# Two transformer blocks on one core: six input slabs and the output projection of the first block in three fp32r passes

## The reference

```
hn = rms_norm(x, norm1_g)
proj = hn @ w_in                      # 1024 x 2304: qa 512, ka 128, va 128, qb 512, kb 512, vb 512
qa, ka = rope(rms_norm(qa)), rope(rms_norm(ka));  qb, kb = rms_norm(qb), rms_norm(kb)
out_a = global_gqa_attention(qa, ka, va)
out_b = dilated_mixture_attention(qb, kb, vb)
mixed = concat([rms_norm(out_a), rms_norm(out_b)])
x = x + mixed @ w_out                 # 1024 x 1024
x = x + conv_ffn(rms_norm(x, norm2_g), w_up, conv_w, conv_b, w_down)
```

## Time and profile before

| | |
|---|---|
| median of 3 runs | 2467.14 us (2466.2 to 2467.89) |
| profiled execution | 2466.14 us, span 2464.4 us |
| mean granted TensorE clock | 0.992 |
| PE busy | 2393.4 us, 97% |
| PEld busy | 2044.9 us, 83% |
| POOL busy | 1603.4 us, 65% |
| DVE busy | 1093.4 us, 44% |
| ACT busy | 1068.3 us, 43% |

### The profile page before, as it was taken

One profiled execution on the slowest core, in us unless ns is written; L12 is line 12 of the kernel. 1 busy time (PEld: TensorE's weight loads), 2 busy tenths in 40 slices (PEclk: granted clock), 3 DMA queues, 4 the chain that ended last, 5 costly groups with the idle time before them and its releaser, 6 DMA issues.

```text
span 2464.4 us, 37279 instructions
## 1 busy us (share of the span) xinstructions
PE 2393.4 (97%) x14828; PEld 2044.9 (83%) x14828; DVE 1093.4 (44%) x2091; ACT 1068.3 (43%) x1987; POOL 1603.4 (65%) x1364
## 2 busy tenths in 40 slices
PE   8999999999999999999999999999998999989998
...
GB/s 219 179 176 193 167 118 126 103 81 195 267 95 131 120 129 119 128 103 180 103 69 103 100 89 103 99 96 98 119 227 122 120 129 136 111 186 158 172 203 137
DMA packets 379311, 339.42 MB, mean 138 GB/s; under 512 B 14448, under 2 KB 343698, under 8 KB 378130
## 3 DMA queue, kind: packets, MB, share of 16 engines
...
q0 software_dynamic: 576, 0.43, 0.2%
...
HBM read 329.62 MB, written 7.61 MB: 137 GB/s over the span
## 4 chain that ended last, share of the span: by engine, by line
PE 87%; POOL 4%; DVE 3%; ACT 2%; issue 2%; DMA 2%; SPq 0%; ACTq 0%; POOLq 0%; DVEq 0%
PE PS L751 41%; PE PS L1167 13%; PE PS L1176 5%; PE PS L809 5%; PE PS L1367 3%; POOL rounded L2824 3%; PE PS L774 3%; PE PS L1224 2%; PE PS L702 2%; PE PS L1081 1%; PE PS L1208 1%; PE PS L1285 1%; PE PS L973 1%; PE PS L1069 1%; DMA ring<-in_w_down_dram 1%
## 5 line engine op out<-in xcount | busy, mean ns | idle before, releaser
L2824 POOL TENSOR_TENSOR rounded<-ring,rounded 128x512 fp32r<-128x512 f32 (+1 forms) x872 | 1115.8, 1313 | 485.0 <-ACT rounded L1419 371.6
L751 PE MATMUL PS<-rounded 128*128 128x256 f32 (+1 forms) x6096 | 1048.1, 334 | 15.7 <-DVE mid_a L2529 5.0
L751 PEld LDWEIGHTS PS<-rounded 128*128 128x128 f32 x6096 | 929.9, 191 | 129.8 <-issue 13.6
L2847 POOL TENSOR_TENSOR rounded<-ring,constants 128x512 fp32r<-128x512 f32 x216 | 230.9, 1099 | 236.4 <-PE PS L751 113.4
L1167 PE MATMUL PS<-rounded 128*128 128x512 f32 (+1 forms) x1536 | 346.8, 382 | 2.3 <-DVE mid_a L2580 1.8
L1167 PEld LDWEIGHTS PS<-rounded 128*128 128x128 f32 x1536 | 274.4, 189 | 58.1 <-issue 6.4
L1419 ACT ACTIVATE rounded<-ring 128x2048 fp32r<-128x2048 f32 (+1 forms) x99 | 180.1, 1823 | 123.9 <-DMA ring<-in_w_mlp_dram 44.4
L2566 DVE SCALAR_TENSOR_TENSOR mid_a<-PS,V,mid_a 128x510 f32<-128x510 f32 (+3 forms) x256 | 182.6, 713 | 71.5 <-ACT mid_a L1764 64.6
L1176 PE MATMUL PS<-rounded 128*128 128x512 f32 (+1 forms) x768 | 140.8, 340 | 0.0
L2029 ACT ACTIVATE PS<-PS 128x512 f32<-128x512 f32 (+1 forms) x64 | 30.4, 475 | 251.7 <-DVE PS L2737 251.6
L1176 PEld LDWEIGHTS PS<-rounded 128*128 128x128 f32 x768 | 117.9, 189 | 18.1 <-issue 3.6
...
## 6 DMA issues: line engine op xcount, KB each, us to landing
ring<-in_w_mlp_dram SPq DMA_DIRECT2D x64, 1024.0 KB, 5.3
ring<-in_w_in_dram SPq DMA_DIRECT2D x56, 1024.0 KB, 5.5
ring<-in_ada_w_dram SPq DMA_DIRECT2D x48, 1024.0 KB, 5.3
...
ring<-in_w_ssd_o_dram SPq DMA_DIRECT2D x16, 1024.0 KB, 5.9
ring<-in_w_out_dram SPq DMA_DIRECT2D x12, 1024.0 KB, 5.0
```

Source lines behind the costliest of these rows:

```text
L751: mm = pe.matmul(PS[:, b, 0:cols], w[:, k, m * P:(m + 1) * P], x(half * kt + k), start=(half == 0 and k == 0 and n_pass == 0), stop=(half ...
L2824: ins = pool.tensor_tensor(lo[:, r], raw[:, r], hi[:, r], ALU.subtract)
L2847: ins = pool.tensor_tensor(hi[:, r], raw[:, r], ones[:, 0:1].broadcast_to([P, 512]), ALU.mult)
```

## The change

The six slabs 4 to 9 of `w_in` go in three passes. POOL splits them by the second form, with two hi buffers in `mid_a`. The normed input is split as well: ACT rounds its eight pieces (`lat_hi`), DVE subtracts (`lat_lo`), and PE waits for these. The four slabs of `w_out` go in three passes too: ACT rounds two of them inside the attention loop, after `exp1` of units 13 and 15, and two in the projection, at k = 1 and 3; POOL subtracts. The turned attention output is rounded by ACT (`mix_hi`), and DVE subtracts (`mix_lo`), which is now what frees the PSUM bank of a transpose. The first two `w_up` slabs are rounded at k = 4 and 5 in place of 3 and 5. A `w_up` slab is free when `split_ready` stands at 10 more than before.

The diff, cut to its core:

```
@@ PE
-            to_features(4, lat, SEQ, act_freed, begin=False, end=False)
+            in_parts = dict(rest=lambda k: lat_lo[:, k, :], hi_at=in_at)
+            pe.wait_ge(*c.need(lo_ready, KT))
+            to_features(4, lambda k: lat_hi[:, k, :], SEQ, act_freed, begin=False, end=False, **in_parts)
...
-            to_tokens(1, 256, LT, act_freed)
+            to_tokens(1, 256, LT, act_freed, parts=(lat_hi, lat_lo), hi_at=in_at)
...
-            to_features(4, lambda k: mix1[:, k, :], SEQ, dve_freed, after=one_behind(hT, SEQ),
-                        first_rows=lambda: pe.wait_ge(*c.need(turned_freed)))
+            def later_mix(k):
+                if k >= KT - 4:
+                    pe.wait_ge(*c.need(turned_freed))
+            to_features(4, lambda k: mix_hi[:, k, :], SEQ, dve_freed, after=one_behind(hT, SEQ), rest=lambda k: mix_lo[:, k, :],
+                        hi_at=out_at, last_rows=later_mix)
@@ ACT
+            for k in range(KT):
+                act.wait_ge(*c.need(scaled))
+                act.activation(lat_hi[:, k, :], hT[:, k, 0:SEQ], ACT.Copy).then_inc(*c.made(hi_ready))
...
             for u in range(n_u + 1):
                 if u < n_u:
                     exp1(u)
+                if u in (n_u - 3, n_u - 1):
+                    round_slab(outs, (u - n_u + 3) // 2, out_at)
                 if u >= 1:
                     weightsT(u - 1, 512)
...
-                turned_to(mix1[:, f, :], SEQ, col("outa_norm_g", f) if f < 4 else col("outb_norm_g", f - 4))
+                turned_to(mix_hi[:, f, :], SEQ, col("outa_norm_g", f) if f < 4 else col("outb_norm_g", f - 4), hi_ready)
...
             for k in range(KT):
+                if k in (1, 3):
+                    round_slab(outs, 2 + k // 2, out_at)
                 square_of_tile(k, hT, SEQ)
-                if k in (3, 5):
-                    round_slab(ups, k // 2 - 1, up_at)
+                if k in (4, 5):
+                    round_slab(ups, k - 4, up_at)
@@ DVE
+            settle(scaled)
+            for k in range(KT):
+                rest_of(lat_lo[:, k, :], hT[:, k, 0:SEQ], lat_hi[:, k, :])
...
             scale_half(1)
+            bank4[0] = 0
+            for f in range(KT):
+                rest_of_turned(mix_lo[:, f, :], mix_hi[:, f, :], col("outa_norm_g", f) if f < 4 else col("outb_norm_g", f - 4), SEQ)
@@ POOL
+            split(range(s0, s0 + 4), in_at)
+            split(range(s0 + 4, s0 + 6), in_at)
+            rests(range(first_slab["out"], first_slab["out"] + 4), out_at)
             rests(up_slabs, up_at, body=FFT, lo_at=(FFT // 2) * up_rest_at)
@@ SP
-                booked((split_ready, j + 1), 2, (tile_ready, total[0] + 2 * (j + 1)))
+                booked((split_ready, 10 + j + 1), 2, (tile_ready, total[0] + 2 * (j + 1)))
```

16 lines of the change are left out of this document (12 added, 4 removed).

## The result

| | before | changed kernel |
|---|---|---|
| median | 2466.67 us (2462.93 to 2467.89) | 2491.16 us (2483.49 to 2499.04) |
| profiled execution | 2466.14 us, span 2464.4 us | 2490.01 us, span 2488.2 us |
| mean granted TensorE clock | 0.992 | 0.984 |

The ratio is 1.0103 [1.0087, 1.0119]: 24.5 us slower between the medians, 21 to 29 by the interval. I had forecast 11.2 us slower, and at most 18. The direction is right, the size is not. A second measurement of the same kernel gave 2489.32 us and 1.0085 [1.0068, 1.0102], so it is not one odd run.

A forecast was written before the change was run, and what follows sets the result against it. PE was taken as the bound, with POOL's 9.2 us pitch now setting the input's end. Input +11.2, attention +3.4, turn +1.15, projection -4.6 made +11.15 us on 2466.14: 2477.3 profiled, 2478.3 median, range 2474.5 to 2485.

The forecast's parts named there:

- POOL sets the end of the input slabs: Input slabs 4 to 9: POOL splits one per 9.2 us, PE needs 5.76 and waits; slab 9 ends 10.3 us later.
- The second chain, by DVE's rotation: Input stage: DVE's rope after slab 7 makes the first maximum at least 9.9 us late, even with slabs 8 and 9 free.
- The waits and the low clock in the input: Input slabs: PE's waits bring 1.2 GHz stretches, costing nothing in the middle, 0.9 us (0 to 1.7) behind the last wait.
- The rule that I cited: Trainium skill: matmul bursts shorter than the operand wait start at the lower clock, so each of six input slabs begins slow.
- ACT's rounding in the attention, 3.4: Attention loop: ACT's rounding of slabs 22 and 23 delays unit 13 and later, last output 3.4 us late (1.9 to 4.6).
- The attention loop as a whole: Attention loop: ACT's rounding of two slabs was the only cost, 3.4 us.
- rival 1: Input slabs: DVE-POOL port costs more than rope rows show, or clock stays low; +17.5 us, 2484.7 (clock: 2483); chance 0.12.
- The turn, +1.15: Turning the attention output: transposes' banks now wait for DVE's subtractions, costing 1.15 us, at most 1.9.
- The projection, -4.6: Output projection: three-pass tiles take 25.8 us in place of 30.4, a gain of 4.6; 3 with waits.
- What follows is shifted as a whole: Everything behind the projection runs on PE and its own waits, moved in time with no change in length.
- the five cases: Whole kernel: the forecast (0.70, 2475 to 2482) and four rivals at 2484.7 (0.12), 2475.4 (0.10), 2481 (0.05), 2460 (0.03).
- Slower: Whole kernel: slower than before by more than the measurable 0.2%, some 5 us; chance 0.95.

The follow-up runs named there:

- e6: Kernel before with only the input slabs in three passes, ACT rounding and POOL only subtracting, four hi buffers, projection in float32: 2465.68 us, 0.9992.
- e3: Changed kernel plus unused matmuls on PE in the waits for the six input splits: 2484.51 us, 1.0072.
- e9: The changed kernel measured again, unchanged: 2489.32 us, 1.0085.
- e7: e2 with POOL's subtractions held until the attention output is scaled, ACT's roundings staying in the loop: 2471.16 us, 1.0013.
- e14: e2 plus 5, 0 and 4 unused matmuls on PE ahead of the weight transposes of units 13, 14 and 15: 2464.11 us, 0.9995.
- e2: Kernel before with only the output projection in three passes, input slabs in float32: 2470.01 us, 1.0024.
- e1: Kernel before with only input slabs 4 to 9 in three passes, output projection in float32: 2478.63 us, 1.0045.

## Why the prediction was wrong

- **POOL sets the end of the input slabs: right for the first profile, and a little dearer.** I had six pitches of 9.2 and 1.2 us for DVE, split at 102.0, 54.6 us behind the first sum of squares. It was 99.85 - 43.29 = 56.6. A start of POOL well before 45 was to be a sign that I was wrong. It began at 42.05, but the first sum of squares was 4.1 us early as well; in the second profile it began at 45.83. Against the first sum of squares it was 0.6 us later than I had it, and its six splits took 57.8 us for 56.4. The two last lines of POOL in the input stage:

```profile
88.24 5.83 POOL L2874 TENSOR_TENSOR rounded<-ring,constants 128x512 fp32r<-128x512 f32 x4
94.14 5.71 POOL L2851 TENSOR_TENSOR rounded<-ring,rounded 128x512 fp32r<-128x512 f32 x4
```

  DVE's rope cost the hi of slab 9 1.8 us and its lo 0.7, not 1.2 over both. With that the stage is 13.1 us longer, for 11.2. e6 shows that the pitch was the main bound: with 5.2 us in place of 9.6 the whole loss is gone. The second chain, by DVE's rotation, I had at 9.9 us against 10.3 and gave it no price. (I had compared the end of the last pair of heads, 108.6, with the old first maximum; like with like it is 10.4, a tie.) In the second profile it ended last, and the stage is 16.5 us longer.
- **The waits and the low clock in the input: right in the first profile, not in the second.** PE waited ahead of slabs 4 to 7 (ahead of slab 8 the rotation had filled the time, ahead of slab 9 the wait for DVE), and the clock fell three times before the last slab without moving the end (e3). My "in the middle they cost nothing" left out that the rotation hangs on slab 7; in e9 that took 2.4 of the 3.4 us by which its input stage is the longer one. The rule that I cited beside it, with each of the six slabs beginning slow, did not hold here: of slabs 4 to 7 two did. It was also no fit: it speaks of bursts shorter than the waits, and I had 5.76 us of work against 3.4 of wait.
- **ACT's rounding in the attention, 3.4: there, and smaller.** Alone it takes 2.3 us (e7), with PE's wait of 2.43 us where I had 2.7; the second rounding was covered.
- **The attention loop as a whole, the step that failed.** The sum had ACT's rounding as the only new thing in the loop. POOL's subtraction, which the rounding starts, runs beside DVE's multiplication of the weights, and that is on PE's path. I had the port in rival 1, but put its whole price on POOL, and only in the input stage. The row I used had POOL stretched by DVE; I never asked for DVE's durations while POOL runs. With ACT's rounding this makes 5.3 us (e14). The second thing left out is the clock: I had it as a price in the input stage and not in the loop, where the waits bring it on and PE's matmuls are on the chain. At the loop's end it is 2.4 us (first profile against second) to 2.8 (e2 against e14). At its start, where PE is busy for 1.13 of 3.10 us behind the late input and then runs 6.9 us at 0.51, it is 2.9 us, read from the times of unit 12; the second profile and e7, each with 3.4 us of low clock there, lose 1.5 and 1.6. Together that is 2.9 + 7.6 = 10.5 us from the first maximum to the turn in the first profile and 1.5 + 5.2 = 6.7 in the second. The first maximum itself came 0.9 to 1.0 us later behind the scores, by DVE.
- **The turn, +1.15: right**, 5.0 us against 3.8.
- **The projection, -4.6: measured -1.8, and -0.5 in the second profile.** Its matmuls run from 172.16 to 199.76, 27.6 us, for 25.8. The first slab took 7.2 us for 5.76, most of it the low clock, and the six tiles behind it 20.4 for 20.1, with a wait of 0.3 for the split of slab 24. The rest is POOL beside DVE again. The norm behind the projection has two small scalings on DVE, 0.48 us together before, with POOL idle:

```profile
201.85 1.59 DVE L2133 TENSOR_SCALAR constants<-constants,stat 128x128 f32<-128x128 f32 x2
...
203.31 0.71 PE L853 MATMUL PS<-constants 128*128 128x128 f32 x4 [1.44 <-DVE constants L2133]
```

  It was 0.34 us before for PE.
- **"What follows is shifted as a whole": wrong in this profile by 3.9 us**, and by 4.0 in the second one. The stage from the feed-forward part to block 2 takes 210.3 to 218.0 us over 16 profiles, and the time at the lower clock in it 3.4 to 17.1 us. A straight line through the 16 points has 208.5 us plus 0.57 per us of low clock, with a correlation of 0.96. Here PE is full, so a low clock costs about half its length, as the earlier trace rows suggested. Over the whole span the clock was low for 80.7 and 72.4 us in the changed kernel, 38.7 before, 49.0 in e1 and 43.1 in e2. Why it had more of it in both its profiles, but not in e3 (49.3), is not settled, and with it why the parts' times do not add up.
- **The rivals.** None of the five cases came out. Rival 1 named the mechanism and missed its side. The range ended at 2485, since I had left the port's price on DVE out of it altogether, and the clock in the loop. "Slower" was right for the reason I gave, POOL's pitch.
